# First mixer: 16 of 29 weight pieces in high and low parts, 14 convolution taps moved from TensorE to GpSimd, and one activation table for Ln and Exp

## The chip, the cores and the metric

The program runs on one core of a Trainium2 chip: TensorE (PE, with its weight loads PEld), VectorE (DVE), ScalarE (ACT), GpSimd (POOL) and the sync engine (SP) that issues the weight transfers. The metric is device time of one execution in microseconds (us); the median of three runs of the kernel before is 2285.95 us (2285.86 to 2286.77).

## What is computed

A stack of blocks on x of 256 tokens by 1024 features, all in float32: `x = x + even_mix(rms_norm(x))`, an expert layer (peer_ffn), `x = x + fox_mix(...)`, a second expert layer, then a block with sliding window attention, spatial gating and a gated MLP. The change is in the first mixer:

```python
def even_mix(h, w_in, conv_w, conv_b, ln_g, ln_b, gate_w2, gate_b, gla_norm_g, w_out):
    p = h @ w_in
    a_val, a_gate, q, k, v, r, glr = jnp.split(p, cuts, axis=-1)
    y_a = conformer_conv(a_val, a_gate, conv_w, conv_b, ln_g, ln_b)
    log_a = jax.nn.log_sigmoid(glr @ gate_w2 + gate_b) / GLA_GATE_TAU
    o = gla_chunked(q, k, v, log_a)
    y_b = rms_norm(o, gla_norm_g) * jax.nn.silu(r)
    return jnp.concatenate([y_a, y_b], axis=-1) @ w_out

def conformer_conv(val, gate, conv_w, conv_b, ln_g, ln_b):
    u = val * jax.nn.sigmoid(gate)          # 512 channels
    y = causal depthwise convolution of u, 31 taps, + conv_b
    return jax.nn.silu(layer_norm(y, ln_g, ln_b))
```

`gla_chunked` is a gated linear attention in chunks of 64 tokens with 4 heads. The kernel computes its inner part by halving: six levels of differences of the cumulated decay (32, 16, ... 1), each giving one masked 128x128 product per head and block.

## The kernel before

Features lie on the 128 partitions, the 256 tokens in the free dimension. Every weight matrix is cut into pieces of 128x1024 float32 (512 KB) that SP loads, in one long order, into a ring of three slots (`ring`). The table `RUNS` names the runs of pieces, their counts and how each is used, its maker:

- WHOLE: PE multiplies the float32 piece itself, 8 matmuls of 256 columns. The slot is free when PE has used it (`pieces_used`).
- POOL or DVE: ACT copies the piece to `w_hi` in the rounded type (`high`, L508), the maker subtracts to get `w_lo` (`low`, L404 for POOL, L1036 for DVE), and PE runs 24 matmuls: high weights by high x and low x, then low weights by high x. The slot is free when the low is done (`lo_pool`, `lo_dve`). x must be in parts too (`xh`, `xl` in `x_parts`).

In the first mixer all 21 pieces of w_in (`ev_in`) and all 8 of w_out (`ev_out`) are WHOLE. The instructions of each engine run in the order in which the code stands; nothing is sorted by a planner. The work of the mixer:

- PE (from L2100): pieces of `ev_in` in pairs (units: bank u mod 3); unit 0 the gate's rank rows, 1 to 4 the convolution's value and gate, 5 q, 6 k, 7 and 8 v (by token), 9 and 10 r. Between units stand the levels (L2143), taps of the convolution's last 128 channels as matmuls with a diagonal (L2153, `last_chunk_taps`, all 31), transposes of e_kd, the chunk sums (L2183), the outputs (L2200, L2203), sums of squares (L2210), then the 8 out pieces (L2230) with the layer norm's two sums (L2238, L2243).
- DVE: evictions of the units, scaled by the root (`scaled`, L1144), q (L1279), decay scans and differences (L1198, L1199), `conv_input` (L1216), the taps of the three other groups of 128 channels (L1226: e_conv = e_u * w + e_conv), `faded` (L1268, L1269), e_kd and e_qb (L1292, L1294), `take` (L1260: predicated copies from the levels' banks into e_at), the chunk states (L1313, L1318), e_o and e_y (L1328, L1334), the layer norm (L1337, L1341), and the addition to x.
- ACT: roots as Exp(-0.5 Ln) (L573, L578), the gates' sigmoids, the fades' Exp (L673), `lay_taps` (L639: the 31 diagonals), the v units (L687), Silu.
- POOL: constants at the start, nothing in the mixer; lows from the first wq piece on.

A function of ACT needs its table; L578 and others show `ACT_TABLE_LOAD` where Ln and Exp follow each other with `preload_act_table(ACT.Ln)`.

Of the kernel before, what the change touches and what calls it, by code (L numbers as in the profile page):

```python
# [7 lines left out]
F32 = mybir.dt.float32  # L8
# [17 lines left out]
EV_ORDER = (0, 5, 6, 9, 10, 7, 8, 11, 12, 1, 2, 3, 4, 17, 18, 19, 20, 13, 14, 15, 16)  # L26
RING = 3
# [37 lines left out]
def build(nc, a, out):  # L65

    ctx = ExitStack()
    with ctx:
# [66 lines left out]
        def b3(ap, n):  # L135
# [102 lines left out]
            ev_gate ev_r ev_chunk_sums ev_states ev_o ev_o_out ev_o_sq ev_o_sum ev_o_root ev_y  # L238
            conv_input conv_step taps_laid conv_mixed ln_sum ln_centred ln_sq ln_var ln_root ln_normed ev_ya
# [13 lines left out]
        RUNS = [("ev_in", "ev_in", 21, WHOLE), ("ev_out", "ev_out", 8, WHOLE),  # L253
# [10 lines left out]
        for name, _, count, who in RUNS:  # L264
            starts[name] = len(maker)
            maker += [who[j % 2] if isinstance(who, tuple) else who for j in range(count)]
# [41 lines left out]
        def _(sp):  # L308
# [64 lines left out]
        def _(pool):  # L373
# [59 lines left out]
            pool.memset(e_at, 0.0).then_inc(g["ev_blank"], 1)  # L433
            for layer in range(2):
# [59 lines left out]
        def _(act):  # L494
# [29 lines left out]
            def raw_norm(k, each, units):  # L524
# [22 lines left out]
                nc.scalar.preload_act_table(ACT.Ln)  # L547
# [86 lines left out]
            laid = [0]  # L634
# [7 lines left out]
            nc.scalar.preload_act_table(ACT.Ln)  # L642
# [10 lines left out]
            roots([(rr, bank[4][:, 0:T])], D, "norm_log", "norm_root", G_EV)  # L653
            act.wait_ge(g["ev_z_in"], 2)
# [36 lines left out]
            v_unit(0)  # L691
            v_unit(1)
            nc.scalar.preload_act_table(ACT.Ln)
# [10 lines left out]
            act.wait_ge(g["units_out"], 11)  # L704
            A(e_r, e_r, ACT.Silu).then_inc(g["ev_r"], 1)
            nc.scalar.preload_act_table(ACT.Ln)

            act.wait_ge(g["ln_centred"], 4)
            A(e_sq2, e_xc, ACT.Square).then_inc(g["ln_sq"], 1)
            act.wait_ge(g["ln_var"], 1)  # L710
# [3 lines left out]
            for c in range(CC):  # L714
                A(e_y[:, (4 + c) * T:(5 + c) * T], e_xn[:, c * T:(c + 1) * T], ACT.Silu, bias=lnb[:, c:c + 1],
                  scale=lng[:, c:c + 1]).then_inc(g["ev_ya"], 1)
            u[0] = 11
# [181 lines left out]
            nc.scalar.preload_act_table(ACT.Ln)  # L899
# [107 lines left out]
        def _(dve):  # L1007
# [314 lines left out]
            three_taps(9, 16)  # L1322
# [1276 lines left out]
```

## Time and profile before

| | |
|---|---|
| median of 3 runs | 2285.95 us |
| span of the profiled execution | 2289.8 us |
| PE busy | 2237.8 us, 98% |
| DVE, ACT, POOL busy | 1559.7, 1212.1, 773.9 us |
| first mixer: first matmul | 7.86 us |
| out pieces of the mixer begin | 118.67 us |
| first expert stage begins on PE | 154.84 us |
| PE waits in the mixer behind its start | 2.6 us (e_y), 0.9 us (e_y's second half) |
| POOL busy from 20 to 140 us | 0 |
| ACT table loads | 40, of 1.283 us |

A timeline row gives start, duration (of a merged group: from its first start to its last end), engine, line, what is written from what, shapes and count, and in brackets the idle time of the engine before it and what ended it. Matmuls of one stream overlap, so their price is read from start to start. A float32 matmul stands as two records.

### The profile page before, as it was taken

To read this page: it belongs to the slowest core of one execution; us is meant where nothing else is said; L and a number is where in the kernel's file an instruction comes from. 1 tells how busy PE (TensorE), PEld (TensorE's weight loads), DVE (VectorE), ACT (ScalarE), POOL (GpSimd) and SP (SyncE) were. 2 spreads that over 40 slices of the span, in tenths; PEclk is the share of its full clock that TensorE was granted. 3 is DMA by queue.
4 is the path that set the end of the run, shared out by engine and by line. 5 is a ranking of instruction groups with operands and counts; after the bars stand their busy time and mean duration, and the time that the engine had idled before them with its cause. 6 is when DMAs were issued, how large, how long until landed. Compare 5 with 4: busy or idle time off the path is not lost.

```text
span 2289.8 us, 43911 instructions
## 1 busy us (share of the span) xinstructions
PE 2237.8 (98%) x14296; PEld 1940.3 (85%) x14296; DVE 1559.7 (68%) x3187; ACT 1212.1 (53%) x1906; POOL 773.9 (34%) x766
## 2 busy tenths in 40 slices
PE   8989999999999999998999999999999999999999
PEld 7879888888888888897998888888888888888877
DVE  6733885888888755544258868888886555435885
ACT  5145556555444455566555555554444555556764
POOL 0027888222323000033778862223320002664000
PEclk9999999999999999998999999999999999999999
DMA  4335655555555566552555655555556665444655
GB/s 159 102 112 163 188 190 175 183 166 174 174 174 171 179 194 192 182 175 93 157 157 186 190 180 169 168 170 176 173 174 185 193 193 175 131 137 150 190 176 164
DMA packets 109649, 385.62 MB, mean 168 GB/s; under 512 B 12512, under 2 KB 14848, under 8 KB 109312
## 3 DMA queue, kind: packets, MB, share of 16 engines
q1 hardware_dynamic: 106864, 382.34, 53.6%
q10 hardware_dynamic: 2704, 2.23, 0.3%
q8 instruction: 47, 0.77, 0.1%
q14 instruction: 34, 0.28, 0.0%
HBM read 383.46 MB, written 1.06 MB: 168 GB/s over the span
## 4 chain that ended last, share of the span: by engine, by line
PE 91%; ACT 3%; DVE 3%; DMA 1%; issue 1%; POOL 1%; SPq 0%; DVEq 0%; ACTq 0%; POOLq 0%
PE bank L1998 23%; PE bank L1978 12%; PE bank L2048 11%; PE bank L2050 11%; PE bank L2049 11%; PE bank L1895 3%; PE bank L1907 3%; PE bank L1899 3%; PE bank L2104 3%; PE bank L2287 3%; PE bank L2230 1%; PE bank L2255 1%; ACT w_hi L508 1%; PE bank L2098 1%; PE bank L2153 1%
## 5 line engine op out<-in xcount | busy, mean ns | idle before, releaser
L508 ACT ACTIVATE w_hi<-ring 128x1024 fp32r<-128x1024 f32 x689 | 727.6, 1057 | 540.6 <-PE bank L2050 403.2
L404 POOL TENSOR_TENSOR w_lo<-ring,w_hi 128x1024 fp32r<-128x1024 f32 x226 | 543.9, 2413 | 809.3 <-ACT w_hi L508 792.8
L1036 DVE TENSOR_TENSOR w_lo<-ring,w_hi 128x1024 fp32r<-128x1024 f32 x463 | 567.6, 1226 | 236.4 <-ACT w_hi L508 230.9
L1998 PE MATMUL bank<-x_parts,w_hi 128*128 128x512 f32 x2320 | 586.2, 394 | 0.2 <-ACT w_hi L508 0.2
L1998 PEld LDWEIGHTS bank<-x_parts,w_hi 128*128 128x128 f32 x2320 | 416.6, 189 | 74.8 <-issue 0.4
L2048 PE MATMUL bank<-w_hi,x_parts 128*128 128x512 f32 x1112 | 439.3, 395 | 0.9 <-DVE x_parts L1043 0.9
L2050 PE MATMUL bank<-w_lo,x_parts 128*128 128x512 f32 x1112 | 433.6, 390 | 0.0
L2049 PE MATMUL bank<-w_hi,x_parts 128*128 128x512 f32 x1112 | 432.6, 389 | 0.0
L1978 PEld LDWEIGHTS bank<-x_parts,w_lo 128*128 128x128 f32 x2368 | 324.7, 190 | 25.3 <-DVE w_lo L1036 3.4
L416 POOL COPY quads<-sco 128x32 f16 (+1 forms) x256 | 169.9, 692 | 514.2 <-DVE sco L1494 514.1
L1978 PE MATMUL bank<-x_parts,w_lo 128*128 128x256 f32 x2368 | 336.8, 283 | 0.2 <-DVE w_lo L1036 0.2
L2050 PEld LDWEIGHTS bank<-w_lo,x_parts 128*128 128x128 f32 x1112 | 208.7, 188 | 44.6
L2048 PEld LDWEIGHTS bank<-w_hi,x_parts 128*128 128x128 f32 x1112 | 208.9, 188 | 43.2 <-DVE w_lo L1036 0.9
L2049 PEld LDWEIGHTS bank<-w_hi,x_parts 128*128 128x128 f32 x1112 | 209.1, 188 | 41.8
L1895 PE MATMUL bank<-x_parts,w_hi 128*128 128x256 f32 x720 | 181.4, 289 | 9.3 <-ACT x_parts L533 7.9
L1899 PE MATMUL bank<-x_parts,w_hi 128*128 128x256 f32 x656 | 160.8, 283 | 0.0
L1895 PEld LDWEIGHTS bank<-x_parts,w_hi 128*128 128x128 f32 x720 | 138.6, 193 | 15.4 <-issue 8.8
L734 ACT ACTIVATE sco<-bank 128x256 f32<-128x256 f32 x136 | 52.2, 384 | 183.8 <-PE bank L1978 183.8
L1486 DVE TENSOR_TENSOR sco<-iota,quads 128x512 f16<-128x512 f16 (+1 forms) x256 | 130.4, 551 | 7.1 <-POOL quads L416 7.1
L1899 PEld LDWEIGHTS bank<-x_parts,w_hi 128*128 128x128 f32 x656 | 125.8, 192 | 0.1
L1043 DVE TENSOR_TENSOR x_parts<-big,x_parts 128x256 fp32r<-128x256 f32 x278 | 116.4, 419 | 0.0
L734 ACT ACTIVATE big<-bank 128x256 f32<-128x256 f32 x120 | 45.9, 384 | 129.0 <-PE bank L1978 129.0
(305 smaller groups left out, 2531.1 us busy)
## 6 DMA issues: line engine op xcount, KB each, us to landing
ring<-u_dram SPq DMA_DIRECT2D x256, 512.0 KB, 3.6
ring<-v_dram SPq DMA_DIRECT2D x256, 512.0 KB, 3.5
ring<-up_dram SPq DMA_DIRECT2D x44, 512.0 KB, 3.7
ring<-wq_dram SPq DMA_DIRECT2D x32, 512.0 KB, 3.6
ring<-sb_in_dram SPq DMA_DIRECT2D x31, 512.0 KB, 3.6
ring<-od_in_dram SPq DMA_DIRECT2D x25, 512.0 KB, 3.6
ring<-down_dram SPq DMA_DIRECT2D x22, 512.0 KB, 4.1
ring<-ev_in_dram SPq DMA_DIRECT2D x21, 512.0 KB, 3.5
```

The costliest lines, as they stand in the source:

```text
L404: pool.tensor_tensor(w_lo[:, k % RING, :], ring[:, k % RING, :], w_hi[:, k % RING, :].bitcast(F32), ALU.subtract).then_inc(g["lo_pool"], 1)
L416: last = pool.tensor_copy(dst[:, at + r], v.to_broadcast([P, GROUP_T, QUAD]))
L508: A(w_hi[:, k % RING, :], ring[:, k % RING, :], ACT.Copy).then_inc(g["w_hi_done"], 1)
L1036: V.tensor_tensor(w_lo[:, k % RING, :], ring[:, k % RING, :], w_hi[:, k % RING, :].bitcast(F32), ALU.subtract).then_inc(g["lo_dve"], 1)
L1486: return V.tensor_tensor(fours(dst), keys.to_broadcast(shape), of_token[:, row].to_broadcast(shape), ALU.is_equal)
L1895: mm(dst, hi[:, rows[c]], xh[:, c, :], start=(c == 0), stop=False)
L1899: mm(dst, hi[:, rows[c]], xl[:, c, :], start=False, stop=False)
L1978: return mm(dst[:, 0:T], lo[:, rows[c]], xh[:, c, :], start=False, stop=False, skip_group_check=True)
L1998: mm(dst[:, :], hi[:, rows[c]], x_both[:, c, :], start=(c == 0), stop=False, skip_group_check=True)
L2048: mm(dst, xh[:, s, t], hi[:, cols], start=False, stop=False, skip_group_check=True)
L2049: mm(dst, xl[:, s, t], hi[:, cols], start=False, stop=False, skip_group_check=True)
L2050: last = mm(dst, xh[:, s, t], lo[:, cols], start=False, stop=False, skip_group_check=True)
```

## The change

`RUNS` makes pieces 0 to 10 of `ev_in` WHOLE and the ten from 11 on POOL, and of `ev_out` the pieces 1, 2, 3, 5, 6, 7 POOL. For that x (`xg`) and e_y are split into high (ACT, `ev_x_hi`, `y_high`) and low (POOL, `ev_low`). The taps 0 to 13 of the last 128 channels go from PE to POOL (`pool_tap`), each after tap 0 as a scaling into `sco` and an addition; the bias goes with tap 0 and DVE adds PE's sum to POOL's. ACT's preload before each root names the set that holds Ln and Exp, so the loads between the two are gone everywhere in the kernel (40 loads before, 23 after). On DVE the eviction of r's first half stands before `take(4)`, that of the second half before the last three taps, and e_y before the convolution's last addition; ACT's Silu of r is in two halves, PE's units of v and r are laid differently among levels and taps.

```diff
+EV_WHOLE = 11
+POOL_TAPS = 14
-        RUNS = [("ev_in", "ev_in", 21, WHOLE), ("ev_out", "ev_out", 8, WHOLE),
+        RUNS = [("ev_in", "ev_in", EV_WHOLE, WHOLE), ("ev_in_b", "ev_in", 21 - EV_WHOLE, POOL),
+                ("ev_out", "ev_out", 8, (WHOLE, POOL, POOL, POOL)),
...
+            def ev_low(src, j, hi_done, done):
+
+                pool.wait_ge(g[hi_done], j + 1)
+                c = slice(2 * j, 2 * j + 2)
+                pool.tensor_tensor(xl[:, c, :], b3(src[:, j * 512:(j + 1) * 512], 2), xh[:, c, :].bitcast(F32),
+                                   ALU.subtract).then_inc(g[done], 1)
+
+            def pool_tap(w):
+
+                c = CC - 1
+                u, y = e_u[:, c * UW + w:c * UW + w + T], b3(e_conv, CC)[:, c, :]
+                if w:
+                    scaled = sco[:, (w % 2) * T:(w % 2 + 1) * T]
+                    step(pool.tensor_scalar(scaled, u, cw[:, w * CC + c:w * CC + c + 1], None, ALU.mult))
+                    settle()
+                    pool.wait_ge(g["conv_pool"], w)
+                    ins = pool.tensor_tensor(y, y, scaled, ALU.add)
+                else:
+                    pool.wait_ge(g["conv_input"], 2)
+                    ins = pool.tensor_scalar(y, u, cw[:, c:c + 1], cb[:, c:c + 1], ALU.mult, ALU.add)
+                ins.then_inc(g["conv_pool"], 1)
+
+            for j in range(4):
+                ev_low(xg, j, "ev_x_hi", "ev_x_lo")
+            k0 = starts["ev_in"]
+            at_tap = 0
+            for k, taps in ((11, 0), (12, 0), (13, 1), (14, 2), (15, 2), (16, 3), (17, 3), (18, 3), (19, 0), (20, 0)):
+                low(k0 + k)
+                for w in range(at_tap, at_tap + taps):
+                    pool_tap(w)
+                at_tap += taps
...
-                nc.scalar.preload_act_table(ACT.Ln)
+                nc.scalar.preload_act_table_set("natural_log_exp_and_others")
...
+            for j in range(4):
+                A(xh[:, 2 * j:2 * j + 2, :], b3(xg[:, j * 512:(j + 1) * 512], 2), ACT.Copy).then_inc(g["ev_x_hi"], 1)
...
             act.wait_ge(g["ev_tables_loaded"], 32)
+            highs(14)
             lay_taps(CONV_W)
+            highs(17)
...
             v_unit(0)
+            highs(19)
             v_unit(1)
-            nc.scalar.preload_act_table(ACT.Ln)
+            highs(21)
+            nc.scalar.preload_act_table_set("natural_log_exp_and_others")
...
             faded(4)
             faded(5)
             three_taps(4, 6)
+            dve.wait_ge(g["units_out"], 9)
+            scaled(e_r[:, 0:512], 9, 19)
             take(4, 3)
             take(5, 4)
             three_taps(6, 8)
-            dve.wait_ge(g["units_out"], 9)
-            scaled(e_r[:, 0:512], 9, 19)
...
-            for _ in range(4):
+            for _ in range(3):
                 whole_unit()
-            whole_unit(by_token=True)
+            pe.wait_ge(g["ev_x_lo"], 4)
+            one_unit(features)
+            token_unit()
             level(0, 6)
             level(1, 0)
-            whole_unit(by_token=True)
+            token_unit()
             level(2, 1)
             level(3, 2)
-            last_chunk_taps(0, 8)
+            one_unit(features)
             level(4, 3)
             level(5, 4)
-            whole_unit()
+            last_chunk_taps(14, 17)
             level(6, 5)
```

In the part left out PE's out pieces 1, 2, 3, 5, 6 and 7 run as 24 matmuls with `xh` and `xl`, which now hold e_y, and the piece lists of ACT's `highs` follow.

On POOL, what stood between the start's constants and the first wq low was nothing. Before (the rows from the last constant on):

```order
L399 MEMSET eps_row 128x1 [waits pool_step]
L433 MEMSET big 128x1024
L423 UNCONDITIONAL_BRANCH
L423 ISA
L404 TENSOR_TENSOR w_lo<-ring,w_hi 128x1024 [waits w_hi_done]
```

After, in the same place (L443 is `ev_low`, L408 `low`, L458, L452 and L455 the taps in `pool_tap`):

```order
L403 MEMSET eps_row 128x1 [waits pool_step]
L437 MEMSET big 128x1024
L443 TENSOR_TENSOR x_parts<-big,x_parts 128x2x256 [waits ev_x_hi] x4
L408 TENSOR_TENSOR w_lo<-ring,w_hi 128x1024 [waits w_hi_done] x3
L458 TENSOR_SCALAR big<-big 128x256 [waits conv_input]
L408 TENSOR_TENSOR w_lo<-ring,w_hi 128x1024 [waits w_hi_done]
L452 TENSOR_SCALAR sco<-big 128x256
L455 TENSOR_TENSOR big<-big,sco 128x256 [waits conv_pool,pool_step]
L452 TENSOR_SCALAR sco<-big 128x256
L455 TENSOR_TENSOR big<-big,sco 128x256 [waits conv_pool,pool_step]
L408 TENSOR_TENSOR w_lo<-ring,w_hi 128x1024 [waits w_hi_done]
```

The fourth low (piece 14) stands behind the first tap, which waits for both halves of the convolution's input; every later low stands behind two or three taps.

On ACT, behind the fades' Exp and the second gate, before:

```order
L676 ACT_TABLE_LOAD
L665 ACTIVATE big<-big 128x512 [waits units_out]
L639 ACTIVATE sco<-ident,big 128x128 [waits ev_tables_loaded]
```

and after (L555 is `high`, L686 `lay_taps`, L738 the first v unit):

```order
L725 ACT_TABLE_LOAD
L714 ACTIVATE big<-big 128x512 [waits units_out]
L555 ACTIVATE w_hi<-ring 128x1024 [waits slot_loaded2,ev_tables_loaded]
L555 ACTIVATE w_hi<-ring 128x1024 [waits slot_loaded0]
L555 ACTIVATE w_hi<-ring 128x1024 [waits slot_loaded1]
L686 ACTIVATE sco<-ident,big 128x128 x17
L555 ACTIVATE w_hi<-ring 128x1024 [waits pieces_used,slot_loaded2]
L555 ACTIVATE w_hi<-ring 128x1024 [waits pieces_used,slot_loaded0]
L555 ACTIVATE w_hi<-ring 128x1024 [waits pieces_used,slot_loaded1]
```

Three highs (pieces 11, 12, 13) now stand ahead of the laying of taps, which has 17 in place of 31, and the high of piece 14 behind it.

## Rows read from the trace of the kernel before

**Rows 1.** Timeline of PE, start us, duration us, idle before in brackets, narrow windows
```profile
28.92 27.79 PE L2104 MATMUL bank<-big,ring 128*128 128x256 f32 x128
...
94.98 0.38 PE L2200 MATMUL bank<-big 128*128 128x128 f32 x2
...
98.44 3.72 PE L2104 MATMUL bank<-big,ring 128*128 128x256 f32 x16
...
109.02 1.88 PE L2210 MATMUL bank<-big,one 128*128 128x512 f32 x4
110.74 5.35 PE L2153 MATMUL bank<-big,sco 128*128 128x256 f32 x24
118.67 5.38 PE L2230 MATMUL bank<-big,ring 128*128 128x256 f32 x16 [2.59 <-DVE big L1334]
...
154.84 0.35 PE L1895 MATMUL bank<-x_parts,w_hi 128*128 128x256 f32 x1 [2.02 <-ACT x_parts L533]
...
166.41 0.28 PE L1895 MATMUL bank<-x_parts,w_hi 128*128 128x256 f32 x1
...
169.29 0.28 PE L1895 MATMUL bank<-x_parts,w_hi 128*128 128x256 f32 x1
```

**Rows 2.** DVE: groups by form, 47 to 94.5 us (two), then its timeline
```profile
L1226 DVE SCALAR_TENSOR_TENSOR big<-big 128x256 f32<-128x256 f32 x52 | 21.3, 480 | 0.0
L1260 DVE COPY_PREDICATED big<-big,bank 128x512 f32<-128x512 int32 x14 | 9.4, 727 | 5.5 <-PE bank L2143 5.4
...
94.99 10.38 DVE L1226 SCALAR_TENSOR_TENSOR big<-big 128x256 f32<-128x256 f32 x26
```

**Rows 3.** Timeline of ACT in the first mixer and at the first wq piece
```profile
21.34 1.28 ACT L578 ACT_TABLE_LOAD   x1
22.63 0.42 ACT L578 ACTIVATE big<-big 128x256 f32<-128x256 f32 x1
...
46.07 9.15 ACT L639 ACTIVATE sco<-ident,big 128x128 f32<-128x128 f32 x31
...
149.46 1.06 ACT L508 ACTIVATE w_hi<-ring 128x1024 fp32r<-128x1024 f32 x1 [9.36 <-DMA ring<-wq_dram]
```

**Rows 4.** POOL and DVE together (timelines); then lines' durations, ns min/median/max
```profile
153.97 2.38 POOL L404 TENSOR_TENSOR w_lo<-ring,w_hi 128x1024 fp32r<-128x1024 f32 x1 [1.03 <-ACT w_hi L508]
...
154.73 1.90 DVE L1077 SCALAR_TENSOR_TENSOR x_parts<-xT,gains,x_parts 128x256 fp32r<-128x256 f32 x1 [1.18 <-ACT x_parts L533]
...
L1077 DVE SCALAR_TENSOR_TENSOR x_parts<-xT,gains,x_parts x40: 472/476/1904, 154.7 to 2094.7; 128x256 fp32r<-128x256 f32 x40
...
L1656 DVE TENSOR_SCALAR big<-big x8: 353/355/2395, 1984.5 to 2030.6; 128x256 f32<-128x256 f32 x8
...
L1107 DVE TENSOR_TENSOR big<-bank,big x24: 678/691/693, 166.0 to 2108.0; 128x512 f32<-128x512 f32 x24
```

**Rows 5.** Timeline of POOL: one-input instructions
```profile
1.79 0.31 POOL L390 MEMSET big<- 128x256 f32 x1
...
1949.40 1.11 POOL L483 TENSOR_SCALAR_AFFINE_SELECT big<-big 128x1024 f32<-128x1024 f32 x1
```

**Rows 6.** Chain of work that ended last, 149 to 153 us
```profile
149.39 3.42 DMA ring<-wq_dram
```

**Rows 7.** Windows: PE, PEld, DVE, ACT, POOL busy, then granted clock
```profile
119.99:123.40 3.41, 3.41 (x10) 2.71 (x9) 0.00 (x0) 0.00 (x0) 0.00 (x0) 0.50 0.00 0
```

**Rows 8.** PE's waits, whole span: us in total, times, longest; then DVE's timeline
```profile
PE bank L2458 <- DVE big L1694: 4.1, 1, 4.1
...
PE bank L1907 <- DVE w_lo L1036: 2.4, 2, 1.6
...
PE bank L2357 <- ACT big L588: 1.5, 1, 1.5
...
PE bank L2406 <- ACT big L872: 1.1, 1, 1.1
...
1970.14 2.38 DVE L1628 SCALAR_TENSOR_TENSOR big<-big,qk_gain 128x512 f32<-128x512 f32 x3 [12.36 <-ACT big L578]
```

More of the change, by code:

```diff
@@ L265, in build @@
             starts[name] = len(maker)
-            maker += [who[j % 2] if isinstance(who, tuple) else who for j in range(count)]
+            maker += [who[j % len(who)] if isinstance(who, tuple) else who for j in range(count)]
         total_pieces = len(maker)
@@ L433, in _ @@
             pool.memset(e_at, 0.0).then_inc(g["ev_blank"], 1)
+            def ev_low(src, j, hi_done, done):
[25 more added lines that the diff above has]
+                at_tap += taps
+            assert at_tap == POOL_TAPS
+            k0 = starts["ev_out"]
+            low(k0 + 1)
+            ev_low(e_y, 0, "ev_y_hi", "ev_y_lo")
+            ev_low(e_y, 1, "ev_y_hi", "ev_y_lo")
+            low(k0 + 2)
+            low(k0 + 3)
+            ev_low(e_y, 2, "ev_y_hi", "ev_y_lo")
+            ev_low(e_y, 3, "ev_y_hi", "ev_y_lo")
+            for j in range(5, 8):
+                low(k0 + j)
             for layer in range(2):
@@ L703, in _, with y_high @@
             roots([(e_orr[:, r * 512:(r + 1) * 512], bank[4 + r][:, :]) for r in range(2)], DV, "ev_o_log", "ev_o_root", 0)
-            act.wait_ge(g["units_out"], 11)
-            A(e_r, e_r, ACT.Silu).then_inc(g["ev_r"], 1)
-            nc.scalar.preload_act_table(ACT.Ln)
+            nc.scalar.preload_act_table(ACT.Silu)
+            for r in range(2):
+                act.wait_ge(g["units_out"], 10 + r)
+                v = e_r[:, r * 512:(r + 1) * 512]
+                A(v, v, ACT.Silu).then_inc(g["ev_r"], 1)
+            nc.scalar.preload_act_table_set("natural_log_exp_and_others")
+            highs(23)
+            def y_high(j, ready, value):
+                act.wait_ge(g[ready], value)
+                A(xh[:, 2 * j:2 * j + 2, :], b3(e_y[:, j * 512:(j + 1) * 512], 2), ACT.Copy).then_inc(g["ev_y_hi"], 1)
+            act.wait_ge(g["pieces_used"], 21)
+            y_high(0, "ev_y", 1)
+            y_high(1, "ev_y", 2)
+            highs(24)
             act.wait_ge(g["ln_centred"], 4)
             A(e_sq2, e_xc, ACT.Square).then_inc(g["ln_sq"], 1)
+            highs(25)
             act.wait_ge(g["ln_var"], 1)
@@ L1329, in _ @@
             settle()
-            dve.wait_ge(g["ev_r"], 1)
+            dve.wait_ge(g["ev_r"], 2)
             for f in range(2):
@@ L2212, in _ @@
             outputs(0)
-            whole_unit(between=lambda: outputs(1))
-            output_sum(0)
-            output_sum(1)
-            last_chunk_taps(19, CONV_W)
+            outputs(1)
+            pe.wait_ge(g["units_out"], 8)
+            for j in range(2):
+                features(unit_bank(u[0])[:, j * T:(j + 1) * T], weights_in_turn(0, 0)).then_inc(g["pieces_used"], 1)
+                n[0] += 1
+                if j == 0:
+                    output_sum(0)
+                    output_sum(1)
+            u[0] += 1
+            last_chunk_taps(24, CONV_W)
             pe.wait_ge(g["units_out"], 11)
```

64 lines of the change are left out of this document (43 added, 21 removed).

## Prediction

> **What bounds the kernel now.** The page first: TensorE (PE) is busy nearly all of the span, so the change pays only where PE does less or waits less. Then PE's timeline in the first mixer [rows 1]. The reader is to see that it runs from 28.92 to 116 us without a gap, waits 2.59 us for VectorE's e_y before the out pieces at 118.67, and 2.02 more before the first expert stage at 154.84. The prices stand there too: a whole piece is 8 float32 matmuls, which the trace holds as 16 records; 128 of them take 27.63 us from start to start (28.92 to 56.55), so 3.45 us a piece. A piece in parts starts 2.88 us after the one before it (166.41 to 169.29), for 24 matmuls. Next VectorE (DVE) in the same stretch [rows 2]: between 47 and 94.5 us it runs 52 conv taps (L1226) and 14 predicated copies, and behind the states 26 more taps in 10.38 us, 0.40 each. Its only long idle there is 5.5 us before the copies, 8 in all: DVE is nearly as full as PE. GpSimd (POOL) does nothing between 4 and 150 us. So last I looked for what happens to DVE when POOL works beside it [rows 4].
>
> **The change part by part.**
>
> *PE does less.* 16 pieces x (3.45 - 2.88) = 9.2 us. 14 of 31 taps leave it; 24 records (12 taps) stand in 5.35 us at L2153, 5.2 without the last one's tail [rows 1], 0.43 a tap, so 6.1 us. Together 15.3 us, all on the path if nothing else comes late.
>
> *ACT* gets 16 highs of 1.06 us and 8 copies of half that size (0.6 each), and loses 14 of its 31 laid taps (9.15 us for 31, 0.295 each) [rows 3]. In the whole kernel 17 of 40 table loads of 1.28 us go. The Trainium skill, "ScalarE: Activation LUTs", What ACT_TABLE_LOAD costs, gives about 2.66 us for a switch, the load and a drain of 1.38. Here the load begins at 21.34 and the Exp at 22.63 [rows 3]: 1.28 is all. By the page the saving behind the mixer, below, would be up to twice as large; the sum goes by the row.
>
> *POOL* gets 16 lows of 2.4 us [rows 4], 8 lows of x and y of half the size (1.2), and 14 taps. A tap is a scaling of 256 columns, bounded by a memset of that size (0.31) and an affine select of 1024 columns (1.11) [rows 5], and an add of 256 columns, a quarter of 2.4 plus a start, 0.65. I take 0.35 for the scaling, as its size is the memset's, and 1.1 for a tap with its two waits. For pieces 11 to 20: 10 x 2.4 + 14 x 1.1 = 39 us.
>
> *What POOL's work does to DVE.* L1077, a scalar_tensor_tensor with two SBUF inputs, took 1.90 us at 154.73, where a POOL low ran from 153.97 to 156.35; it ended 0.28 after the low. Its median is 0.476. L1656 took up to 2.395 instead of 0.355, a whole low. L1107, which reads PSUM and SBUF, stays within 0.678 and 0.693 in all 24, POOL or not [rows 4]. So a DVE instruction with two SBUF inputs stands until POOL's instruction is over, and where both queue they alternate. Of that kind are the conv taps (e_u and e_conv), the fades, e_kd, e_qb, conv_input, e_o and e_y; not of that kind are the scaled evictions, e_q, the predicated copies (one input in PSUM) and the states. The Trainium skill, "GPSIMD Engine Reference", Key points, says that GpSimd shares its SBUF interfaces with VectorE and contends with its instructions in a 2-port mode or with two SBUF inputs. The trace agrees (1.90 for 0.48). It is the rule that speaks against this change.
>
> *The walk through the mixer*, with these prices; a piece lands 3.42 us after its slot is free [rows 6].
> PE reaches piece 11 at 28.92 + 6 x 3.45 = 49.64 as before; piece 11 lands at 46.2, 12 at 49.6, 13 at 53.1, and high and low of each are in time. Then ACT lays 17 taps (5.0 us), so the high of piece 14 comes at 60.15, and PE waits 2 us for it. DVE is 1.3 us early from the missing loads, but must wait for piece 10 for e_q. Lows 11, 12 and 13 hold it for some 2 us each, so conv_input(1) ends at 60.0. POOL's first tap stands behind that, low 14 behind the tap (63.5). PE ends piece 14 at 64.5 and gets e_k at 65.2.
> From here DVE and POOL alternate. POOL: 2 taps and low 15 (ends 69.7), 2 taps and low 16 (75.7), 3 taps and low 17 (82.9), 3 taps and low 18 (90.9), 3 taps and lows 19 and 20 (99.7). DVE does one instruction of 0.35 between two of POOL's, so its first predicated copy comes at 78.8; PE waits 3.5 us for it and 3.6 for low 18. From 100 on POOL is quiet, PE waits for DVE, and DVE's states are ready at 115.2; before, the taps behind them began at 94.99. A cross-check: 39 us of POOL are added, of which at most 20 can lie under DVE's waits (8), its predicated copies (9.4) and its other PSUM work (3). So 94.6 + 39 - 20 = 113.6 is the floor.
> From 115.2 PE leads: both outputs 2 x 3.5 (94.98 to 98.44 for one), piece 19 2.9, sums 1.75; then ACT's Ln, Exp, Silu load and Silu to 131.9, DVE's e_o and the first e_y to 133.6. Before, e_y was there at 118.67: 15 us late, where PE's work alone is 12 us shorter.
> The tail from there is two whole pieces, six in parts and two sums of 1.75: 6.9 + 17.3 + 3.5 = 27.7, to 161.4; before it took 34.1, to 152.8. POOL's lows free ring slots earlier than PE did, so wq's first pieces are there, and PE's idle of 2.02 becomes 0.9: the experts start at 162.3, before at 154.84. **Mixer: +7.5 us**, +6 from the floor. The clock went to half for 3.41 us at 119.99, right after PE's idle of 2.59 [rows 7]; the new mixer has more and longer idles of PE, for which I add 1.0, between 0 and 3.
>
> *Behind the mixer* only table loads change; they count where ACT's chain ends last [rows 8]. In the second mixer PE waits 1.1 us at L2406 and 1.5 at L2357, both behind a busy ACT; six loads (7.7 us) go there, and 1.1 + 1.0 = 2.1 come free (the last eviction stays). L1907 waits twice for DVE's lows, 1.6 and 0.8, behind a root that is now 1.28 earlier: 1.3 + 0.8 = 2.1. L2458 waits 4.1 for L1694; three loads (3.8) leave the chain ahead of it, but DVE's L1628 (to 1972.52) stands in front, held by a POOL low, so L1694 starts only 1.8 earlier. **Sum: -6.0.**
>
> Total: +7.5 + 1.0 - 6.0 = +2.5 us on the profiled span of 2289.8, and the same on the median 2285.95, which is 3.85 lower: **2288.5 us**.
>
> **The rivals.**
> A, the forecast: the two engines alternate, the mixer ends late, the saved loads pay most of it back. Chance 0.48; own range 2282 to 2296 (5 us of error in the walk, 0 to 3 of clock).
> B, faster: DVE's taps are not held. Then POOL's lows alone pace PE: pieces 14, 16, 18 end at 63.6, 72.8, 84.2, the outputs start at 93.3, e_y is there at 111.6, the experts start at 140.2: -14.6 - 6.0 = -20.6, 2265 us. For it: the held rows are few and of other stages. Against it: L1077 has the tap's form. Chance 0.14.
> C, slower: the predicated copies are held as well, since mask and target lie in SBUF. Then their 9.4 us [rows 2] hide nothing and the states come at 124: 2288.5 + 9 = 2297.5. It decides from the point where a copy beside a low takes over 1 us instead of 0.73. A scaling of 1.0 us on POOL, near the affine select, costs the same (14 x 0.65). Chance 0.22.
> D, milder: POOL's short tap instructions slip into DVE's gaps and half of its exposed 19 us is hidden: -9 from the mixer, 2279 us. Chance 0.16.
>
> **How the numbers follow.** A measurement tells about 0.2% (4.6 us) from no change. Faster: B and D less 0.02 of it, with 0.01 of A: 0.29. Slower: C and 0.10 of A: 0.32. Same: 0.39. The range leaves out B and the far end of C: 2270 to 2298.
>
> **What would show it.** Right: DVE taps of 1 to 2.7 us between 47 and 100; PE waits of 3 us and more for the first predicated copies and for low 18; outputs starting near 115, experts near 162; 2.2 us left of the idle before L2458. Wrong: taps that keep 0.48 us and outputs near 93 (B); predicated copies over 1 us, or POOL taps over 1.7 (C); POOL's instructions stretched and DVE's not (D).

## The result, and the profile after

The changed kernel takes 2296.7 us (median of 4 runs, 2295.59 to 2297.27), the kernel before 2285.9 (4 runs, 2285.43 to 2286.77). The ratio is 1.0042, with a 95% interval of 1.003 to 1.0053: slower by 10.8 us. The forecast was 2288.5 with a range of 2270 to 2298. The range holds the time, near its end; "no difference that can be told" was the likeliest outcome, and that was wrong: it is the third, slower by more than 0.2%, which had 0.32. The time lies just above the forecast case's own range too (A, 2282 to 2296). A run's time is some 2 us more than its span; the profiled execution of after is one of these four, that of before, with a span of 2289.8, was some 6 us longer than the timed runs. What that does is told below, under the profiled execution of before.

The head of after's page: span, then busy time and share of each engine.

```profile
span 2293.6 us, 44206 instructions
...
PE 2228.9 (97%) x14396; PEld 1938.2 (85%) x14396; DVE 1592.4 (69%) x3187; ACT 1206.0 (53%) x1899; POOL 849.7 (37%) x817
```

The first mixer decides, and there TensorE's timeline (start, duration, idle before it in brackets), which answers to [rows 1]. L2005 and L2012 are pieces 13 to 16 by token, L1965 to L1977 pieces by feature, L2272 the outputs, L2223 the taps, L2310 a whole out piece.

```profile
61.31 0.38 PE L2005 MATMUL bank<-w_hi,x_parts 128*128 128x256 f32 x1 [2.02 <-ACT w_hi L555]
...
70.84 1.22 PE L2012 MATMUL bank<-w_lo,x_parts 128*128 128x256 f32 x8 [1.39 <-POOL w_lo L408]
...
77.72 2.06 PE L2012 MATMUL bank<-w_lo,x_parts 128*128 128x256 f32 x8 [3.74 <-POOL w_lo L408]
...
85.98 1.22 PE L1977 MATMUL bank<-x_parts,w_lo 128*128 128x256 f32 x8 [1.43 <-POOL w_lo L408]
...
94.37 2.08 PE L1977 MATMUL bank<-x_parts,w_lo 128*128 128x256 f32 x8 [5.26 <-POOL w_lo L408]
...
111.78 0.67 PE L2272 MATMUL bank<-big 128*128 128x128 f32 x2 [4.99 <-DVE eps_row L1389]
...
124.08 0.58 PE L1965 MATMUL bank<-x_parts,w_hi 128*128 128x256 f32 x1
...
129.19 1.88 PE L2282 MATMUL bank<-big,one 128*128 128x512 f32 x4
...
137.92 2.40 PE L2310 MATMUL bank<-big,ring 128*128 128x256 f32 x10 [0.96 <-DVE big L1401]
...
167.15 0.36 PE L1965 MATMUL bank<-x_parts,w_hi 128*128 128x256 f32 x1 [1.21 <-POOL w_lo L408]
```

What ran without a gap to 116 us before now waits 2.0 us for the high of piece 14, 1.4, 3.7, 1.4 and 5.3 for lows 15 to 18, and 5.0 for VectorE's states (L1389 is the mark behind them). The experts start at 167.15 instead of 154.84.

Two views say why. First VectorE and GpSimd side by side, in two places (predicated copies, L1328, and conv taps), then GpSimd's groups by form between 40 and 110 us (busy us, mean ns), with VectorE's conv taps (L1294), which were L1226 with a mean of 480 ns in [rows 2].

```profile
82.90 2.75 DVE L1328 COPY_PREDICATED big<-big,bank 128x512 f32<-128x512 int32 x4
83.54 2.38 POOL L408 TENSOR_TENSOR w_lo<-ring,w_hi 128x1024 fp32r<-128x1024 f32 x1
...
90.16 1.09 DVE L1294 SCALAR_TENSOR_TENSOR big<-big 128x256 f32<-128x256 f32 x2
...
92.04 2.56 DVE L1294 SCALAR_TENSOR_TENSOR big<-big 128x256 f32<-128x256 f32 x1
...
89.94 1.10 POOL L452 TENSOR_SCALAR sco<-big 128x256 f32<-128x256 f32 x1
91.11 0.72 POOL L455 TENSOR_TENSOR big<-big,sco 128x256 f32<-128x256 f32 x1
91.80 2.52 POOL L408 TENSOR_TENSOR w_lo<-ring,w_hi 128x1024 fp32r<-128x1024 f32 x1
...
L408 POOL TENSOR_TENSOR w_lo<-ring,w_hi 128x1024 fp32r<-128x1024 f32 x10 | 24.9, 2494 | 21.9 <-ACT w_hi L555 21.9
L452 POOL TENSOR_SCALAR sco<-big 128x256 f32<-128x256 f32 x13 | 15.5, 1189 | 0.0
L455 POOL TENSOR_TENSOR big<-big,sco 128x256 f32<-128x256 f32 x13 | 9.8, 755 | 1.1
...
L1294 DVE SCALAR_TENSOR_TENSOR big<-big 128x256 f32<-128x256 f32 x63 | 43.4, 755 | 0.0
```

A conv tap that meets a low stands for 2.56 us. In one of GpSimd's scalings (L452, one input) two conv taps find room, 1.09 us for both. The four predicated copies, which read PSUM, beside a low take 2.75 us together, each the 0.73 of [rows 2].

Second, TensorE by windows: busy time of PE, PEld, DVE, ACT and POOL, then the granted clock (and DMA).

```profile
77.70:98.30 20.60, 13.90 (x106) 12.93 (x108) 17.55 (x27) 4.24 (x5) 19.93 (x19) 0.75 0.38 128
98.30:111.80 13.50, 8.51 (x83) 6.68 (x81) 13.12 (x25) 0.60 (x1) 6.06 (x4) 1.00 0.25 78
111.80:124.10 12.30, 12.30 (x41) 9.57 (x41) 9.34 (x24) 1.23 (x2) 0.00 (x0) 0.50 0.00 1
124.10:137.00 12.90, 12.86 (x67) 11.18 (x66) 3.03 (x5) 7.07 (x10) 0.00 (x0) 0.81 0.00 0
```

The clock is at half (1.2 of 2.4 GHz) for half of the time between 77.7 and 98.3, and again through both outputs and piece 19. [Rows 7] showed 3.41 us of this before.

### The profile page after: what moved, and what is told of

The parts are those of the page before. It is cut to its first block, busy times and chain, and to the rows that moved or that the text cites. A ratio compares the mean times of both kernels' runs of the same rounds, so it can differ in the third digit from the quotient of the medians.

```text
span 2293.6 us, 44206 instructions
## 1 busy us (share of the span) xinstructions
PE 2228.9 (97%) x14396; PEld 1938.2 (85%) x14396; DVE 1592.4 (69%) x3187; ACT 1206.0 (53%) x1899; POOL 849.7 (37%) x817
## 4 chain that ended last, share of the span: by engine, by line
PE 91%; DVE 4%; POOL 2%; ACT 1%; issue 1%; DMA 1%; SPq 0%; DVEq 0%; ACTq 0%; POOLq 0%
PE bank L2068 23%; PE bank L2048 12%; PE bank L2118 11%; PE bank L2120 11%; PE bank L2119 11%; PE bank L1965 3%; PE bank L1977 3%; PE bank L1969 3%; PE bank L2382 3%; PE bank L2174 2%; DVE big L1294 1%; POOL w_lo L408 1%; PE bank L2350 1%; DVE x_parts L1145 1%; POOL sco L452 1%
## 5 line engine op out<-in xcount | busy, mean ns | idle before, releaser
L555 ACT ACTIVATE w_hi<-ring 128x1024 fp32r<-128x1024 f32 x705 | 744.3, 1057 | 562.9 <-PE bank L2120 402.4
L408 POOL TENSOR_TENSOR w_lo<-ring,w_hi 128x1024 fp32r<-128x1024 f32 x242 | 584.2, 2421 | 709.4 <-ACT w_hi L555 694.0
L2068 PEld LDWEIGHTS bank<-x_parts,w_hi 128*128 128x128 f32 x2320 | 416.6, 189 | 74.8 <-issue 0.4
L1965 PE MATMUL bank<-x_parts,w_hi 128*128 128x256 f32 x768 | 195.5, 291 | 8.5 <-ACT x_parts L580 5.9
L1969 PE MATMUL bank<-x_parts,w_hi 128*128 128x256 f32 x704 | 173.9, 284 | 0.0
L1965 PEld LDWEIGHTS bank<-x_parts,w_hi 128*128 128x128 f32 x768 | 148.9, 194 | 14.8 <-issue 8.0
L1969 PEld LDWEIGHTS bank<-x_parts,w_hi 128*128 128x128 f32 x704 | 136.1, 193 | 0.4 <-issue 0.2
```

The lines of the kernel that those rows point to most:

```text
L408: pool.tensor_tensor(w_lo[:, k % RING, :], ring[:, k % RING, :], w_hi[:, k % RING, :].bitcast(F32), ALU.subtract).then_inc(g["lo_pool"], 1)
L555: A(w_hi[:, k % RING, :], ring[:, k % RING, :], ACT.Copy).then_inc(g["w_hi_done"], 1)
L1965: mm(dst, hi[:, rows[c]], xh[:, c, :], start=(c == 0), stop=False)
L1969: mm(dst, hi[:, rows[c]], xl[:, c, :], start=False, stop=False)
L2068: mm(dst[:, :], hi[:, rows[c]], x_both[:, c, :], start=(c == 0), stop=False, skip_group_check=True)
```

## The experiments

Three theories were put to the test. **Theory 1**: work of GpSimd with two inputs holds VectorE's instructions with two SBUF inputs, and the states come late. **Theory 2**: only the lows, late on their way from ScalarE over GpSimd, cost time. **Theory 3**: TensorE's idles halve its clock, and that is what the forecast lacked. The kernel before was run in each round too (median 2287.5, 2287.3 and 2288.3 us beside the three groups of runs, 2283.2 to 2294.0); the ratio to it is the measure, and a time expected before is set against the ratio times 2285.9.

**Beside the kernel before, dummy work on GpSimd.** From the fifth unit on it does nothing but this, and nobody reads it:

```diff
+            step(pool.memset(w_lo[:, :, :].bitcast(F32), 0.0))
+            settle()
+            pool.wait_ge(g["units_out"], 5)
+            for k in range(16):
+                step(pool.tensor_tensor(w_lo[:, 2, :], w_lo[:, 0, :].bitcast(F32), w_lo[:, 1, :].bitcast(F32), ALU.subtract))
+                settle()
```

> The kernel before, and beside its first mixer GpSimd does 16 subtractions of 128x1024 with two inputs (2.4 us each, some 39 us, from the fifth unit on, near 46 us), whose results nobody reads. Everything else is as before. Theory 1 (an instruction of VectorE with two SBUF inputs stands until GpSimd's is over): conv taps of L1226 take up to 2.4 us, VectorE is late by 39 less what lies under its waits and PSUM work (at most 20), states near 110 to 114 instead of 94.6, experts start 13 to 19 us later, total 2299 to 2305. Theory 2 (only the lateness of lows that TensorE waits for costs time): nobody waits for these, so taps keep 0.48 us and the total is 2286. Theory 1b (predicated copies held too): 2308 or more.

Measured: 2316.5 us, ratio 1.0127 (1.0103 to 1.0151), which is +29 us. For the next two the loop's body is a memset (41 times), and a tensor_scalar with one input (16 times).

> As the run with 16 dummy subtractions, but GpSimd does 41 memsets of 128x1024 (no input at all, about 1 us each by 0.31 for a quarter of the size, some 40 us in all). If any work of GpSimd holds VectorE, this costs as much as the subtractions in sum (2299 to 2305), with taps of about 1 to 1.4 us. If only GpSimd's reading with two inputs holds it, 2286 and taps of 0.48.

Measured: 2287.1 us, ratio 1.0001 (0.9988 to 1.0015).

> The kernel before, and beside its first mixer GpSimd scales 16 times 1024 columns with one input (L452 took 1.1 us for 256 columns in the trace of after, so 3 to 4 us each, some 50 to 60 us in all); nobody reads the results. In the trace of after two conv taps of VectorE ran within one such scaling. If one-input work does not hold VectorE: taps of 0.48 us, total as before, 2286 to 2288. If it does: as the dummy subtractions, which took 2316.

Measured: 2291.5 us, ratio 1.0014 (1.0003 to 1.0025). The groups by form between 40 and 110 us (subtractions, memsets, scalings, each time GpSimd's work and VectorE's conv taps), and TensorE's wait beside the subtractions:

```profile
L438 POOL TENSOR_TENSOR w_lo<-w_lo 128x1024 fp32r<-128x1024 f32 x16 | 38.6, 2410 | 41.5 <-DVE big L1150 40.3
L1232 DVE SCALAR_TENSOR_TENSOR big<-big 128x256 f32<-128x256 f32 x50 | 53.3, 1132 | 0.0
91.03 3.78 PE L2149 MATMUL bank<-big 64*128 64x128 f32 x32 [26.12 <-DVE big L1150]
...
L438 POOL MEMSET w_lo<- 128x1024 f32 x41 | 39.2, 956 | 41.0 <-DVE big L1150 38.7
L1232 DVE SCALAR_TENSOR_TENSOR big<-big 128x256 f32<-128x256 f32 x90 | 36.5, 478 | 0.1
...
L438 POOL TENSOR_SCALAR w_lo<-w_lo 128x1024 fp32r<-128x1024 f32 x16 | 46.7, 2920 | 40.6 <-DVE big L1150 39.4
L1232 DVE SCALAR_TENSOR_TENSOR big<-big 128x256 f32<-128x256 f32 x90 | 43.5, 554 | 0.1
```

The same 39 us of GpSimd cost 29 us of the kernel with two inputs and nothing with none. With one input a conv tap's mean goes from 0.478 to 0.554, 7 us over 90 taps, and 3 us of the total (0.7 to 5.7 by the interval). It is a milder hold: by the trace nine taps, each of which began 0.1 to 0.4 us behind the start of a scaling of 2.9, took 1.25 us, and the others kept 0.47, but for one of 0.68. Theory 1 stands, theory 2 can't explain a loss where nobody waits for GpSimd. The price was above my 13 to 19: VectorE got hardly more than one conv tap done in each 2.5 us, and since TensorE ran out of work behind it (26 us), VectorE's own waits, which I had counted as cover, were no longer there to cover anything.

**The table alone.** Before, with the three preloads of Ln changed to the common set:

```diff
-                nc.scalar.preload_act_table(ACT.Ln)
+                nc.scalar.preload_act_table_set("natural_log_exp_and_others")
```

> The kernel before with the one table for Ln and Exp alone; the mixer's pieces, taps and order are untouched. My step 'table loads behind the mixer -6.0' gives 2280 us by the median, with another 1.3 if the first mixer's e_y comes earlier by the load that its root loses: 2278.6. The trace of after, read against before, shows a lead of only 4.4 us won back between the first expert stage and the end once before's half-clock stretch at 1052 is taken out (4.1 us): by that 2280 to 2281.5. Rival: the loads are hidden anyway and what after won behind the mixer was only that clock stretch: then 2285 to 2286, and PE's idles of 1.11 (L2406), 1.5 (L2357) and 1.6 (L1907) stay.

Measured: ratio 0.9985 (0.9974 to 0.9997), so -3.4 us, between -0.7 and -5.9. Faster, less than forecast, and short of both numbers given (by the ratio 2282.5, between the theory's 2280 to 2281.5 and the rival's 2285 to 2286). The two waits of TensorE in the second mixer that the rival wanted to stay, L2406's and half of L2357's, went.

**The parts without GpSimd's taps.** After, with POOL_TAPS = 0: TensorE and ScalarE have all 31 taps again.

> The kernel after with all 31 taps back on TensorE and ScalarE; the 16 pieces in parts, their lows by GpSimd and the order of r stay. It takes from GpSimd 14 scalings (1.1 us each) and 14 additions of 256 columns (0.75 each, which hold a conv tap of VectorE as the lows do). Theory 1 (VectorE held by two-input work paces the mixer): 14 holds of some 0.5 us less, states 7 to 10 us earlier than after's 111; TensorE has 6 us more of taps, but idles 19 us here anyway: total 2284 to 2290. Theory 2 (the lateness of lows alone): lows 14 to 18 come 2 to 13 us earlier, so TensorE hardly waits and the 9.2 us of the parts come through: 2274 to 2278. If TensorE's work is what counts: 2302.

Measured: 2286.3 us, ratio 0.9997 (0.9986 to 1.0008), or 2285.2: theory 1's range, and 10 us faster than after with 6 us more work on TensorE. Its timeline at the two waits that count:

```profile
65.30 0.58 PE L2005 MATMUL bank<-w_hi,x_parts 128*128 128x256 f32 x1 [6.17 <-ACT w_hi L555]
...
102.53 0.46 PE L2272 MATMUL bank<-big 128*128 128x128 f32 x2 [1.05 <-DVE eps_row L1389]
```

TensorE hardly waits for a low any more (0.3 us), and the outputs still start at 102.5 instead of before's 94.98 [rows 1], behind VectorE: ten lows hold it. The 6.17 us are the 31 taps that ScalarE lays ahead of a high.

**The taps without the parts.** Before with the table and the 14 taps on GpSimd, all pieces whole.

> The kernel before with the one table, and the 14 taps on GpSimd; all pieces whole, no lows, order of r as before. Against the run with the table alone TensorE loses 6.1 us of taps. Theory 1: the 14 additions hold VectorE 0.3 to 0.7 us each (4 to 10 us), of which its waits for TensorE take some 5: states and TensorE about even, 2277 to 2283. Theory 2 (no hold): 6 us under the table-only kernel, 2277 or less. With VectorE's lateness fully on the path: 2285 or more.

Measured: 2285.0 us, ratio 0.9983 (0.9971 to 0.9996), the same as the table alone to within 0.0002. The six us that TensorE saves are lost: it idles 2.41 us for the states, and behind that idle its clock goes to half for 10.24 us. By the ratio it is 2282.0, within theory 1's 2277 to 2283 and 5 us above theory 2's.

**After, with TensorE's idles filled.** Three runs. First its last seven taps ahead of the wait for the states:

```diff
-            last_chunk_taps(19, 24)
+            last_chunk_taps(19, CONV_W)
...
-            last_chunk_taps(24, CONV_W)
```

> The kernel after with one move: TensorE's last seven taps (24 to 30), which stand behind the r pieces, go ahead of its wait for the states. They then fill 3 of the 5.0 us that it idles at 107 to 111.8. Theory 3 (the stretch of half clock of 17.07 us from 111.9 on follows from that idle, and is the larger part of my error): with 2 us left the clock stays full, and the outputs to e_y take 18 to 20 us instead of 26: 3 us from the taps and up to 7 from the clock, 2287 to 2290 by the median. Rival: the clock falls anyway (idles earlier in the mixer do it, or the idle that is left): only the 3 us of taps, or less, 2293.5 to 2296.7.

Measured: 2296.7 us, ratio 1.0047 (1.0031 to 1.0064). No gain; the idle ahead of the outputs was 0.74 us, and the clock fell all the same, in four stretches of together 27.3 us, as much as in after. From the outputs to e_y it took 23.2 us instead of 26.1, but then TensorE, whose taps were done, idled 3.98 us for e_y, and the first out piece ran at half clock. The rival. Then matmuls with zeros in each wait (the edit shows those ahead of the states; four lows have 9, 26, 9 and 36):

```diff
+            for _ in range(34):
+                mm(bank[3][:, T:2 * T], zeros[:, :], ident[:, :].bitcast(BF16), start=False, stop=False, skip_group_check=True)
             pe.wait_ge(g["ev_level_in"], 14)
             pe.wait_ge(g["ev_states"], 1)
```

> The kernel after, and in five of TensorE's waits (lows 15 to 18 and the states) it multiplies by a matrix of zeros, into a free half of a bank or adding nothing to the taps: 9, 26, 9, 36 and 34 matmuls of 256 bf16 columns (0.13 us each from start to start), some 0.2 to 0.9 us less in each wait than it idles there. Theory 3 (the idles of TensorE are what halves its clock, for 27.3 us in the mixer of after, and that is what my sum lacked): the stretches at 77.8, 91.4 and 111.9 go, outputs to e_y take 19 to 21 us instead of 26.1, total 4 to 8 us less: 2289 to 2293. Rival: the clock falls all the same, or TensorE at half clock only ate into its own waits: 2296 to 2298.

Measured: 2296.7 us, ratio 1.0041 (1.0024 to 1.0058), or 2295.3: no gain that the intervals can tell, and nearer the rival. The stretches ahead of 100 us are gone, the one behind the states is not.

> The kernel after with the same fillings of zeros as in the run before of this kind, but 56 instead of 34 matmuls ahead of the states. With 34 TensorE still idled 2.81 us before its outputs and the clock was at half from 112.16 for 17.07 us; both outputs took 12.0 us. 22 more at 0.114 us each leave 0.3 us. Theory 3a (that last idle starts the stretch): the clock stays full, both outputs take 7.0 us, piece 19 2.9 instead of 5, and the total falls by 6 to 7.5 us, to 2289 to 2291. Rival 3b (the outputs' own small matmuls, not the idle, bring the clock down): half clock again near 112, total 2296 to 2298.

Measured: 2293.7 us, ratio 1.0025 (1.0014 to 1.0035). The windows: 77.7 to 98.3 and 111.8 to 124.1 with 34 fillings, the latter with 56, and the start of the outputs there.

```profile
77.70:98.30 20.60, 17.24 (x168) 15.56 (x169) 19.02 (x30) 4.24 (x5) 19.93 (x20) 1.00 0.37 128
...
111.80:124.10 12.30, 12.30 (x42) 9.67 (x43) 9.20 (x24) 1.57 (x3) 0.00 (x0) 0.51 0.00 0
...
111.80:124.10 12.30, 11.89 (x52) 9.83 (x52) 9.79 (x26) 2.46 (x4) 0.00 (x0) 0.68 0.00 1
...
112.28 0.46 PE L2280 MATMUL bank<-big 128*128 128x128 f32 x2 [0.41 <-DVE eps_row L1389]
```

Three things follow. With full clock between 77.7 and 98.3 the states came at 111.65 instead of 111.78: half clock there had cost nothing, as VectorE set the time. With 2.81 us of idle left ahead of the outputs the clock was at half for both of them; with 0.41 it fell 3.9 us into them, for 10.24 us instead of 17.07, and the kernel took 3 us less. So the idle accounts for part of the loss, and something in the outputs for the rest; both expectations for this run were too clean, 3a and 3b.

**The parts with ScalarE's taps laid apart.**

```diff
-            lay_taps(CONV_W)
-            highs(17)
+            lay_taps(8)
+            highs(15)
+            lay_taps(8)
+            highs(16)
+            lay_taps(CONV_W)
+            highs(17)
...
-            last_chunk_taps(14, 19)
+            last_chunk_taps(14, 22)
```

> The kernel after without taps on GpSimd (16 pieces in parts, 31 taps on TensorE, 2286.3 by its own run), with two moves: ScalarE lays the 31 taps around the highs of pieces 14 to 16 (8, 8, 15) instead of all ahead of them, which took 9.1 us and made TensorE idle 6.17 us at 65.3; and three of the taps behind the r pieces go ahead of the wait for the states, 1.3 us where TensorE idles 1.05 and its clock fell at 106.76 for 10.24 us. If VectorE, held by ten lows, paces the states, the first move brings 0 to 2 us and the second 3 to 5 by the clock: 2280 to 2284. If TensorE paces, 6 us and more: 2276 to 2280. If the states come later or no earlier and the clock falls anyway: 2285 to 2287.

Measured: 2285.4 us, ratio 0.9992 (0.998 to 1.0004), or 2284.1: at the upper end of the first expectation (2280 to 2284), and no gain over the run before that the intervals can tell. The wait for the high is gone, and in its place stands one of 4.26 us for VectorE at 67.19. The outputs started at 103.41 with no idle at all ahead of them, and the clock fell at 109.16, for 6.83 us. This profiled execution was one of the longer ones of its kernel (2290.3 us).

**Only the out pieces in parts**, which stand where VectorE has little to do: before with the table, and with RUNS as

```diff
-        RUNS = [("ev_in", "ev_in", 21, WHOLE), ("ev_out", "ev_out", 8, WHOLE),
+        RUNS = [("ev_in", "ev_in", 21, WHOLE), ("ev_out", "ev_out", 8, (WHOLE, POOL, POOL, POOL)),
```

and what goes with it on ScalarE, GpSimd and TensorE, as in the change.

> The kernel before with the one table, and of the 29 pieces only six, of the out projection, in high and low parts with lows by GpSimd; the 21 in pieces whole, all taps on TensorE. Here VectorE has little to do but the mean and variance steps, so a hold costs little. 6 x 0.57 = 3.4 us less on TensorE; after ran this tail in 28.0 us where before took 34.1. Expected against the table-only kernel 3 to 6 us less: 2278 to 2281. Rival: the lows of y stand before the parts (1.2 us each, two of them) and hold the centring steps, so that TensorE waits 2 to 4 us for the second piece: no gain, 2282 to 2284.

Measured: 2283.8 us, ratio 0.9985 (0.9973 to 0.9996). By the time no gain over the table alone, and 2282.5 by the ratio is the rival's number, but not its mechanism: TensorE did not wait for the second piece. The experts start 1.3 us earlier in the trace (151.26 instead of 152.56), though 3.41 us of half clock stand in this mixer and none in that of the table alone. Behind the mixer the lead is lost again, above all at 966.53, where TensorE waits 1.80 us for a high and with the table alone does not. What VectorE's timeline shows ahead of the out pieces the next run takes up:

```diff
-            dve.wait_ge(g["conv_mixed"], 1)
-            V.tensor_scalar(cv[:, CC - 1, :], bank[3][:, T:2 * T], cb[:, CC - 1:CC], None, ALU.add).then_inc(g["conv_step"], 1)
             dve.wait_ge(g["ev_o_root"], 2)
...
+            dve.wait_ge(g["conv_mixed"], 1)
+            V.tensor_scalar(cv[:, CC - 1, :], bank[3][:, T:2 * T], cb[:, CC - 1:CC], None, ALU.add).then_inc(g["conv_step"], 1)
             dve.wait_ge(g["ln_sum"], 1)
```

> The kernel before with one table and the six out pieces in parts, and one step of VectorE moved: the bias of the last tap chunk (which waits for TensorE's last tap, 115.9) goes behind e_o and e_y instead of ahead of them. There the root is ready at 113.0 and the Silu at 115.4, so the first e_y is ready near 116 instead of 118.4, and TensorE's wait of 2.59 us before the out pieces falls to 0.2 or less, so that the clock's half stretch at 119.75 (3.41 us) goes too. Expected 2.4 to 4 us under the run without the move: 2279.5 to 2281.5 by the median, experts starting near 148.5. Rival: ScalarE's Silu, not VectorE's order, sets e_y: no gain.

Measured: 2279.8 us (5 runs, 2278.18 to 2281.18), ratio 0.9964 (0.995 to 0.9978). The two timelines, without the move and with it: e_o, e_y, and TensorE's first out piece.

```profile
116.29 1.28 DVE L1359 SCALAR_TENSOR_TENSOR big<-big 128x1024 f32<-128x1024 f32 x1
117.60 3.45 DVE L1365 TENSOR_TENSOR big<-big 128x512 f32<-128x512 f32 x2
118.44 2.48 PE L2263 MATMUL bank<-big,ring 128*128 128x256 f32 x8 [2.59 <-DVE big L1365]
...
114.77 1.28 DVE L1357 SCALAR_TENSOR_TENSOR big<-big 128x1024 f32<-128x1024 f32 x1 [3.36 <-ACT big L596]
117.21 1.29 DVE L1363 TENSOR_TENSOR big<-big 128x512 f32<-128x512 f32 x2 [1.15 <-ACT big L723]
118.05 3.69 PE L2263 MATMUL bank<-big,ring 128*128 128x256 f32 x16 [0.47 <-DVE big L1363]
```

Without the move the second e_y was held by the low of the next piece (3.45 us for the two). With it both take 1.29, the idle of 2.59 is 0.47, and no half clock is seen in the mixer. That the shorter idle is what spared it is not shown: the table alone idled the same 2.59 us and has none either. By its median this run lies in the range expected, by the ratio (2277.7) below it. It beats both kernels: 8 us, by the ratio, under before and 18 under after; against the table alone it is 4.8 us, with intervals that just touch. Of the gain over the run before, 4.8 us by the ratios, the two traces show 1.6. In the mixer it is more than the starts of the experts (150.19 and 151.26) say, since the stream of whole pieces that [rows 1] shows from 28.92 on began at 30.41 us here and at 28.68 there: from its start to the experts it is 2.8 us less, of which some 1.7 are the half clock. The rest lies in which execution was profiled: that of the run before was 2.3 us under its median, and its five longest executions show a mean granted clock of 0.994 to 0.996, where the five of this run show 0.996 to 0.999.

## Why the forecast came out as it did

**The profiled execution of before.** Beside its span of 2289.8, the run with memsets, where VectorE and TensorE do the same work with the same durations, spans 2283.2, which fits the timed runs. The difference is two stretches of half clock and a wait. The windows of the second mixer, in before and in the run with memsets:

```profile
1040.00:1066.00 26.00, 22.05 (x150) 19.02 (x150) 9.72 (x46) 18.47 (x52) 12.70 (x7) 0.80 0.27 82
...
1040.00:1066.00 26.00, 21.89 (x187) 18.50 (x185) 14.32 (x66) 20.48 (x65) 11.10 (x7) 1.00 0.26 81
```

Before was at half clock for 10.24 us there, after was not; the run with 16 scalings and the one with the taps laid apart were again. So it comes and goes, and costs some 4.2 us. The other stretch is that of [rows 7]: 3.41 us at 119.99, worth 1.7 us, which the run with memsets does not have, although TensorE idled the same 2.59 us ahead of its out pieces (they took 3.69 us instead of 5.38). The wait of 1.6 us at L1907 [rows 8] was not in the run with memsets either (0.9 at most). Read against that run, after starts its experts 14.0 us late (167.15 to 153.13) and ends 10.4 late (2293.6 to 2283.2), which is about the 10.8 of the medians; read against before's own trace it would be 12.3 and 3.8. The forecast was +8.5 and +2.5. A time within one trace also carries its start: the stream of pieces that [rows 1] shows from 28.92 on began at 28.84 us in the run with memsets and at 29.79 in after, and in all the traces between 28.7 and 30.7, so that some 0.9 of the 14.0 were there before the changed pieces began.

**PE does less, ACT**: as reckoned; a piece in parts starts 2.88 us after the one before it, and ACT's high of piece 14 made PE wait 2.02 us (forecast 2).

**POOL's prices.** Lows 2.49, forecast 2.4. A tap's scaling took 1.19, where I took 0.35 by the size of the memset; the affine select's 1.11 [rows 5] was the near row. With the addition (0.755) a tap is 1.9 us, over the 1.7 that the forecast had set as a sign of rival C, whose second way was a scaling of 1.0. So this part of C came true. GpSimd had 51 us to do instead of 39, low 18 came at 94.3, not at 90.9, and PE waited 5.3 us for it, not 3.6. That C's 2297.5 lies next to the measured 2296.7 is luck all the same: C put its 9 us on the states, and they came earlier than forecast, not later.

**The hold.** Right in kind (conv taps of 2.56 us) and in its exceptions: the 14 predicated copies kept their 0.73 us in after, where eight of them ran beside a low, and beside the memsets and the scalings. (Beside the dummy subtractions none ran: GpSimd was done at 86.7 us and they began at 95.8.) So rival C's first way, held copies, is excluded, and so is rival B. The Trainium skill, "GPSIMD Engine Reference", Key points, names VectorE's two SBUF inputs as the condition; the conv taps agree beside subtractions (1132 ns instead of 480), and don't beside memsets (478). Too strict in one point: I let VectorE have one instruction between two of GpSimd's, whatever they were, and a scaling lets two pass, which is a little of rival D. The two errors run against each other. The states came at 111.7; the walk said 115.2, its floor 113.6. The holding work alone, 24.9 + 9.8 = 34.7 us, less the 20 us of cover, gives 109.3, an estimate. PE did not wait for the first predicated copies, where I had 3.5 us. This step was 3.5 us too dear.

**The clock is the term that was mis-sized.** From the outputs to e_y I had 18.4 us, and it took 26.1. The outputs took 12.3 us instead of 7.0, piece 19 5.1 instead of 2.9, both at half clock: 7.5 us, where the forecast had 1.0 and a bound of 3. I had taken the bound from [rows 7], 3.41 us behind an idle of 2.59, though the same walk had PE wait three times for 3 us and more; the fillings took back 2.9 of it (outputs to e_y in 23.2 us), and the kernels with half clock in this place all have states later than TensorE or both outputs in a row. The tail, 28.0 against 27.7, and the idle before the experts, 1.2 against 0.9, were right. So 162.3 (without the clock) became 167.15: -3.4, +7.7, +0.6.

**Behind the mixer**: -6.0 was forecast, -3.6 came (14.0 less 10.4), and the table alone shows the same 3.4 between its experts and its end. Of the second mixer's heads (L2406, L2357) 1.9 came of 2.1. Two rows that I built on did not carry. L1907's wait of 1.6 was peculiar to that execution. And at L2458, where I expected 1.8, PE's idle (L2553 in after) stayed: 4.4 us, 4.1 before. The timelines of VectorE and GpSimd there, which answer to the last of [rows 8]:

```profile
1972.21 5.90 DVE L1698 SCALAR_TENSOR_TENSOR big<-big,qk_gain 128x512 f32<-128x512 f32 x3 [11.03 <-ACT big L625]
1978.04 1.40 DVE L1764 SCALAR_TENSOR_TENSOR big<-big 128x512 f32<-128x512 f32 x2
...
1971.73 2.42 POOL L408 TENSOR_TENSOR w_lo<-ring,w_hi 128x1024 fp32r<-128x1024 f32 x1 [2.24 <-ACT w_hi L555]
1974.66 2.91 POOL L408 TENSOR_TENSOR w_lo<-ring,w_hi 128x1024 fp32r<-128x1024 f32 x1 [0.51 <-ACT w_hi L555]
```

Without the loads ScalarE finishes its roots and the next high earlier, so GpSimd's next low starts at 1974.66, and L1698's third instruction, ready at 1975.29, stands until 1978.11 behind it: three take 5.90 us instead of 2.38. So the same hold ate the saved loads here too, and the run with the table alone has the same 5.90 us. The Trainium skill, "ScalarE: Activation LUTs", What ACT_TABLE_LOAD costs, has 2.66 us for a switch where the row has 1.28; by it my -6.0 would have been up to twice as large, an estimate. The runs do not bear that out: 3.4 and 3.6 lie on the other side of the row's price. I had named one low in this place and not asked what the earlier high would start.

**The sum.** Against the undisturbed before: mixer +14.0 (forecast 8.5), behind it -3.6 (forecast -6.0). Both miss on the same side, 7.9 us together. Of the 5.5 in the mixer, 3.9 are the steps above (4.9, less the 1.0 allowed for the clock), and 1.7 the half clock at 119.99, which I took for a part of before and which its undisturbed execution does not have. Without the 3.4 us by which the states came earlier than forecast, the clock would have put the time beyond the range: that the range held owes something to errors of opposite sign. The signs of all steps were right; the classes were decided by a term that I priced at 1 us from a single row.

What stays open: what in the outputs brings the clock down where nothing idles ahead of them. In before one whole piece stands between outputs(0) and outputs(1), and in those of its kin that idle 0.7 us or less ahead of them no half clock is seen there; after puts them in a row, and every kernel with that order has it, with 0 to 5 us of idle ahead. That the order is the cause is argued, not shown: after with the piece between them was not run.

## What to carry to other kernels

An engine that is free isn't free to use: ask first whether its instructions read two operands while another engine's next ones do too. Put such work where the other engine waits anyway (the six out pieces, which paid only with VectorE's order changed too), not where it is as full as the bound (the ten in pieces), and when a step is made shorter, follow what its engine starts next. Where a change makes TensorE wait, price the work behind the wait at half clock and put that in the range, and compare with more than one execution of before.

## What the runs showed of the hardware

- A two-input GpSimd instruction holds a VectorE instruction with two SBUF inputs for its whole length, at 256 columns (0.75 us) as at 1024 (2.5 us). A memset of 1024 columns holds nothing (480 and 478 ns a tap), and 16 scalings of 1024 cost VectorE about 7 us, 0.4 us each. The predicated copies, with one input in PSUM, kept 0.73 us beside lows, memsets and scalings.
- GpSimd's scaling of 256 columns took 0.9 to 1.9 us, mostly 1.1, more than its addition of two inputs (0.75).
- Half clock in TensorE's records began inside idles of 3.7 to 26 us or up to 1.4 us into the work behind idles of 2.0 to 5.0 us. It does not follow every idle: behind the same 2.59 us ahead of the out pieces it came in before, in the run with scalings and in that with the out pieces in parts, and not with the table alone, the subtractions or the memsets. In outputs(0) and (1) in a row it also came behind 0 to 1.05 us of idle, 2.8 to 5.8 us after their start.
- Of the 27 us at half clock in after between 60 and 137 some 7.5 were lost, since only those behind the states lay on the path.
